# Gate and up of two SwiGLU feed-forwards as seven half products, all of down behind them

## The reference, cut to what matters

```python
def rmsnorm(x, g):
    xf = x.astype(jnp.float32)
    y = xf * lax.rsqrt(jnp.mean(xf * xf, axis=-1, keepdims=True) + EPS)
    return (y * g.astype(jnp.float32)).astype(x.dtype)

def swiglu(h, w_gate, w_up, w_down):
    return (jax.nn.silu(h @ w_gate) * (h @ w_up)) @ w_down

    x = x + 0.5 * swiglu(rmsnorm(x, g_ffn1), w1_gate, w1_up, w1_down)
    ...
    x = x + 0.5 * swiglu(rmsnorm(x, g_ffn2), w2_gate, w2_up, w2_down)
```

## Time and profile before

| what | value |
|---|---|
| median of three runs | 2342.95 us |
| time of the profiled execution | 2342.71 us |
| its span in the profile | 2340.9 us |
| PE busy in the span | 2311.1 us, 99% |
| DVE, ACT, POOL busy | 1217.3, 593.6, 59.9 us |
| moved by DMA | 169.23 MB, mean 72 GB/s |

### The profile page before, as it was taken

The page is one execution under the profiler, slowest core; times in us unless marked ns, Lnnn a source line. Parts: engine busy times, 40 slices in busy tenths (PEclk is TensorE's granted clock), DMA queues, the critical chain, the costliest instruction groups (busy, mean ns, idle before and its releaser), DMA issues.

```text
span 2340.9 us, 37286 instructions
## 1 busy us (share of the span) xinstructions
PE 2311.1 (99%) x15084; PEld 2247.2 (96%) x15084; DVE 1217.3 (52%) x2337; ACT 593.6 (25%) x1020; POOL 59.9 (3%) x100
## 2 busy tenths in 40 slices
PE   8999999999999999999999999999999999999999
PEld 7999999999999999986899987999999999999998
DVE  6544444444445775466878345265444444444445
ACT  6111211111112332246623033141111111111112
POOL 0000000000000000012400000000000000000000
PEclk9999999999999999999999999999999999999999
DMA  4111111111111321157533334311111111111111
GB/s 149 40 51 36 54 36 54 54 36 54 36 54 37 117 56 43 32 155 237 176 115 118 119 127 145 111 37 54 38 54 36 54 54 36 49 41 48 41 36 75
DMA packets 185421, 169.23 MB, mean 72 GB/s; under 512 B 6659, under 2 KB 165137, under 8 KB 185065
## 3 DMA queue, kind: packets, MB, share of 16 engines
q1 hardware_dynamic: 185329, 167.94, 23.1%
HBM read 147.98 MB, written 20.04 MB: 72 GB/s over the span
## 4 chain that ended last, share of the span: by engine, by line
PE 61%; DVE 1%; ACT 0%; DMA 0%; issue 0%; SPq 0%; DVEq 0%; ACTq 0%
PE bank L2281 17%; PE bank L2282 17%; PE bank L2283 17%; PE bank L2882 1%; PE bank L2894 1%; PE bank L2986 1%; PE bank L2715 1%; PE bank L2914 1%; PE bank L2777 1%; PE bank L2781 1%; PE bank L2787 0%; PE bank L2651 0%; DMA out_mem_k_prompt_dram<-kst 0%; PE bank L2903 0%; PE bank L2936 0%; PE bank L2924 0%
## 5 line engine op out<-in xcount | busy, mean ns | idle before, releaser
L2281 PE MATMUL bank<-h_hi,w_hi 128*128 128x352 f32 x3120 | 1011.4, 324 | 5.8 <-DVE h_lo L1361 2.8
L2282 PE MATMUL bank<-h_lo,w_hi 128*128 128x352 f32 x3120 | 1000.6, 321 | 0.0
L2283 PE MATMUL bank<-h_hi,w_lo 128*128 128x352 f32 x3120 | 1000.5, 321 | 0.0
L2281 PEld LDWEIGHTS bank<-h_hi,w_hi 128*128 128x128 f32 x3120 | 586.0, 188 | 8.4 <-DVE w_lo L1332 3.2
L2282 PEld LDWEIGHTS bank<-h_lo,w_hi 128*128 128x128 f32 x3120 | 587.3, 188 | 0.0
L2283 PEld LDWEIGHTS bank<-h_hi,w_lo 128*128 128x128 f32 x3120 | 585.8, 188 | 0.0
L1426 DVE SCALAR_TENSOR_TENSOR x<-bank,x 128x352 f32<-128x352 f32 x528 | 276.3, 524 | 187.5 <-PE bank L2283 187.3
L2281 PE MATMUL bank<-mid_hi,w_hi 128*128 128x352 f32 x1056 | 341.3, 323 | 1.2 <-DVE x L1426 1.2
L2282 PE MATMUL bank<-mid_lo,w_hi 128*128 128x352 f32 x1056 | 338.3, 320 | 0.0
L2283 PE MATMUL bank<-mid_hi,w_lo 128*128 128x352 f32 x1056 | 338.0, 320 | 0.0
L1332 DVE TENSOR_TENSOR w_lo<-w_raw,w_hi 128x1024 fp32r<-128x1024 f32 x190 | 231.1, 1244 | 48.1 <-ACT w_hi L864 46.1
(11 more groups left out here) (333 smaller groups left out, 1436.6 us busy)
## 6 DMA issues: line engine op xcount, KB each, us to landing
w_raw<-in_w_gate_dram SPq DMA_DIRECT2D x44, 512.0 KB, 3.9
w_raw<-in_w_up_dram SPq DMA_DIRECT2D x44, 512.0 KB, 4.7
w_raw<-in_w_down_dram SPq DMA_DIRECT2D x44, 512.0 KB, 4.0
w_raw<-in_w_in_dram SPq DMA_DIRECT2D x18, 512.0 KB, 4.6
x_spill<-x SPq DMA_DIRECT2D x6, 1408.0 KB, 6.2
kring<-in_cache_mem_k_dram SPq DMA_DIRECT2D x8, 1024.0 KB, 5.3
vring<-in_cache_mem_v_dram SPq DMA_DIRECT2D x8, 1024.0 KB, 5.3
dec<-acs_row SPq DMA_DIRECT2D x8, 768.0 KB, 6.5
```

The lines of the kernel that those rows point to most:

```text
L2281: eng.matmul(out, a_hi, b_hi, start=first, stop=False)
L2282: eng.matmul(out, a_hi, b_lo, start=False, stop=False)
L2283: return eng.matmul(out, a_lo, b_hi, start=False, stop=last)
```

## The change

**Seven products.** The normalised operand H (1024 features by 1056 rows) is cut in two by features and in two by rows, and each pair of weight tiles (two tiles of 128 output features, called a chunk as before) in two by input features and in two by output tile. That is a 2 x 2 by 2 x 2 block product, done in seven block products where there were eight. Each half of the rows is 528 columns, too wide for a PSUM bank of 512, so a product is made in two quarters of 264 columns (`TQ`). Products 1 to 7 of gate and of up are issued in the order `STEADY` in chunks 1 to 9, in `OPENING` in chunk 0 and `CLOSING` in chunk 10. Products 2, 3 and 6 are accumulated onto the PSUM contents of another product, so some products wait until ACT or DVE has copied a value out.

**Weights.** A chunk's gate weights are two raw tiles, and so are its up weights (four raw buffers now). GpSimd makes the weight sums in place (`sums_13`, `sums_24`); unit A is a raw tile, B and C are raw tiles whose halves were replaced by sums, D is one more half tile (128 x 512). ACT makes the high parts (`g_hi`) and DVE the low ones (`g_low`), 7 tiles' worth per chunk in place of four for gate and up.

**Operands.** The sums of halves of H need it fully normalised: x is written to DRAM (`x_keep`), GpSimd multiplies it by gain and factor in place (`normalise`, `rescale`), ACT and DVE split it, and DVE and GpSimd form the sums of halves (`second_half`, `s3_sum`). The first product no longer starts on x that isn't normalised. x is read back at the end of the products.

**Combining.** ACT copies product 1 out (`take_p1`), DVE combines the others (`take_w`, `take_u`, `take_21`, `take_12`), ACT applies the silu, GpSimd multiplies gate by up for three of the four blocks (`multiply`), DVE for the first (`act_11`). The result of every chunk is written to DRAM (`act_keep`) in four DMAs.

**Down.** All 11 chunks of down follow behind the products of all 11. Their activations are read back, ACT makes `mid_hi` and GpSimd `mid_lo` (`low_mid`). Number and shape of the down matmuls are as before (144 of 352 columns per chunk).

```diff
+HT, TQ, KH = T // 2, T // 4, KT // 2
+LAST = CHUNKS - 1
+HALF_K = KH * P
+GATE, UP = 0, 1
+ORDER = ((GATE, 1), (GATE, 2), (UP, 1), (UP, 2), (GATE, 5), (GATE, 7), (GATE, 6), (GATE, 4), (GATE, 3),
+         (UP, 5), (UP, 7), (UP, 6), (UP, 4), (UP, 3))
+STEADY = [(m, p, t) for m, p in ORDER for t in range(2)]
+OPENING = [(m, p, t) for t in range(2) for p in (1, 2) for m in (GATE, UP)] + [
+    (m, p, t) for m, p in ((GATE, 4), (UP, 4), (GATE, 5), (GATE, 7), (GATE, 6), (GATE, 3), (UP, 5), (UP, 7), (UP, 6), (UP, 3))
+    for t in range(2)]
...
-        mid_hi = sb("mid_hi", "MID", 22528, [P, 2, T], F32R)
-        mid_lo = sb("mid_lo", "MID", 30976, [P, 2, T], F32R)
-        gate = sb("gate", "MID", 39424, [P, 2, TN])
-        prod = sb("prod", "MID", 42240, [P, 2, TN])
...
+        def free(f, c, kind, m):
+            last = max(order.index((m, p, 1)) for order in (OPENING, STEADY)
+                       for p in {"A": (2,), "D": (6,), "B": (5, 4), "C": (7, 3)}[kind])
+            return NPROD * chunks(f, c) + last + 1
...
+            def act_out(f, c, q_):
+                n = chunks(f, c)
+                if q_ == 0:
+                    eng.wait_ge(g_mix, mixed(f, c, "act11", UP, 1))
+                else:
+                    eng.wait_ge(g_act, 6 * n + 2 * q_)
+                half, fi = ((0, 0), (1, 1), (1, 0), (0, 1))[q_]
+                a = slice(HT * half, HT * half + HT)
+                eng.dma_start(act_keep[:, bass.ds(2 * c + fi, 1), a], act[:, fi:fi + 1, a]).then_inc(s_act, 16)
...
+            def sums_13(f, c, m):
+                n = chunks(f, c)
+                w0, w1 = wg[2 * m], wg[2 * m + 1]
+                eng.wait_ge(g_rdy, prepared(f, c, "A", m))
+                eng.wait_ge(g_dma[m], 32 * (n + 1))
+                eng.tensor_tensor(w0[:, 0:HALF_K], w1[:, 0:HALF_K], w0[:, 0:HALF_K], ALU.subtract).then_inc(g_sum, 1)
+                eng.tensor_tensor(w1[:, 0:HALF_K], w1[:, HALF_K:2 * HALF_K], w1[:, 0:HALF_K], ALU.subtract).then_inc(g_sum, 1)
...
+            def sums_24(f, c, m):
+                n = chunks(f, c)
+                w0, w1 = wg[2 * m], wg[2 * m + 1]
+                if not (isinstance(c, int) and c == 0):
+                    eng.wait_ge(g_prod, free(f, c - 1, "D", m))
+                eng.wait_ge(g_sum, 8 * n + 2 * m + 2)
+                eng.tensor_tensor(d_f[:, m, :], w1[:, HALF_K:2 * HALF_K], w0[:, 0:HALF_K], ALU.subtract).then_inc(g_sum, 1)
+                eng.wait_ge(g_sum, 8 * n + 4 + 2 * m + 1)
+                eng.tensor_tensor(w0[:, HALF_K:2 * HALF_K], d_f[:, m, :], w0[:, HALF_K:2 * HALF_K], ALU.subtract)\
+                   .then_inc(g_sum, 1)
...
+            def multiply(f, c):
+                n = chunks(f, c)
+                for j, (half, fi, step) in enumerate(((1, 1, "22"), (1, 0, "21"), (0, 1, "12"))):
+                    eng.wait_ge(g_evict, evicted(f, c, "silu", GATE, j))
+                    for t in range(2):
+                        u_ = (p522[t][:, :], first_p[UP][:, t, :], wsum[:, t, :])[j]
+                        eng.wait_ge(g_mix, mixed(f, c, step, UP, t))
+                        out = quarter(act, half, fi, t)
+                        eng.tensor_tensor(out, u_, out, ALU.mult).then_inc(g_act, 1)
...
+            def first_half(f, t):
+                for n in range(t + 1):
+                    eng.wait_ge(s_spill[n], (16, 64)[f])
+                a, b = TQ * t, TQ * t + TQ
+                normalise(f, 0, KT, a, b, 26 * f + 10 * t)
+                eng.wait_ge(x_rb, (t + 1, spread_at(4, t) + 1)[f])
+                rescale(0, a, b)
+                rescale(KH, a, b)
...
+            def second_half(f):
+                for n in (1, 2):
+                    eng.wait_ge(s_spill[n], (16, 64)[f])
+                normalise(f, 0, KH, HT, T, 26 * f + 20)
+                eng.wait_ge(x_rb, (3, spread_at(4, 2) + 1)[f])
+                rescale(0, HT, T)
...
+            def low_mid(f, c, parity):
+                for n in range(NT):
+                    eng.wait_ge(f_mh, 3 * chunks(f, c) + n + 1)
+                    eng.tensor_tensor(mid_lo[mids(c, parity)][:, :, cols(n)], mid_raw[parity][:, :, cols(n)],
+                                      mid_hi[mids(c, parity)][:, :, cols(n)].bitcast(F32), ALU.subtract).then_inc(f_ml, 1)
...
+            def take_p1(f, c, m, t):
+                n = chunks(f, c)
+                if m == GATE:
+                    wait(eng, g_mix, mixed(f, c, "21", GATE, 1) - len(MIX))
+                else:
+                    wait(eng, g_act, 6 * n)
+                eng.wait_ge(g_prod, done(f, c, m, 1, t))
+                eng.activation(first_p[m][:, t, :], p_bank(f, m, 1, t)[:, 0:TQ], ACT.Copy).then_inc(g_evict, 1)
...
+            def silu_11(f, c, t):
+                wait(eng, s_act, 64 * chunks(f, c))
+                eng.wait_ge(g_prod, done(f, c, GATE, 2, t))
+                eng.activation(quarter(act, 0, 0, t), p_bank(f, GATE, 2, t)[:, 0:TQ], ACT.Silu).then_inc(g_evict, 1)
...
+            def strassen_chunk(f, c):
+                for t in range(2):
+                    take_p1(f, c, GATE, t)
+                for t in range(2):
+                    silu_11(f, c, t)
+                if not (isinstance(c, int) and c == 0):
+                    g_hi(f, c, "C", UP)
+                for t in range(2):
+                    take_p1(f, c, UP, t)
+                for m in range(2):
+                    g_hi(f, c + 1, "A", m)
+                strassen_rest(f, c)
...
+            def strassen_rest(f, c):
+                silu(f, c, 0)
+                g_hi(f, c + 1, "D", GATE)
+                silu(f, c, 1)
+                g_hi(f, c + 1, "B", GATE)
+                silu(f, c, 2)
+                g_hi(f, c + 1, "C", GATE)
+                g_hi(f, c + 1, "D", UP)
+                g_hi(f, c + 1, "B", UP)
...
+            def take_w(f, c, m, t):
+                eng.wait_ge(g_prod, done(f, c, m, 7, t))
+                eng.wait_ge(g_evict, evicted(f, c, "p1", m, t))
+                if m == GATE:
+                    wait(eng, g_act, 6 * chunks(f, c))
+                eng.tensor_tensor(wsum[:, t, :], first_p[m][:, t, :], p_bank(f, m, 7, t)[:, 0:TQ], ALU.subtract).then_inc(g_mix, 1)
...
+            def strassen_chunk(f, c):
+                if not (isinstance(c, int) and c == 0):
+                    g_low(f, c, "C", UP)
+                    for t in range(2):
+                        act_11(f, c, t)
+                for m in range(2):
+                    g_low(f, c + 1, "A", m)
+                combine(f, c, GATE)
+                for kind in "DBC":
+                    g_low(f, c + 1, kind, GATE)
+                combine(f, c, UP)
+                for kind in "DB":
+                    g_low(f, c + 1, kind, UP)
...
-            def ffn_gate(f, i, t):
-                gi, n = 66 * f + t + 6 * i, TURNS[t][1]
-                eng.wait_ge(f_g, gi + 1)
-                wait(eng, f_p, gi - 1)
-                eng.tensor_tensor(gate[:, t % 2, :], bank[t % 2][:, 0:TN], rb[:, cols(n)], ALU.mult).then_inc(f_gs, 1)
...
+            def product(f, c, m, p, t):
+                kind = {1: "A", 2: "A", 5: "B", 4: "B", 7: "C", 3: "C", 6: "D"}[p]
+                opening = isinstance(c, int) and c == 0
+                if t == 0:
+                    eng.wait_ge(g_rdy, prepared(f, c, kind, m))
+                if opening and f and (m, p) in ((UP, 1), (GATE, 4)):
+                    eng.wait_ge(p_free, (125 if p == 4 else 123) + t)
+                before = not opening or f
+                if (m, p) == (UP, 1) and before:
+                    eng.wait_ge(g_mix, mixed(f, c, "12", UP, t) - len(MIX))
+                elif p == 4 and before:
+                    eng.wait_ge(g_mix, mixed(f, c, "21", m, t) - len(MIX))
+                elif p == 2:
+                    eng.wait_ge(g_evict, evicted(f, c, "p1", m, t))
+                elif (m, p) == (GATE, 5):
+                    eng.wait_ge(g_evict, evicted(f, c, "silu11", GATE, t))
+                elif (m, p) == (GATE, 7):
+                    eng.wait_ge(g_mix, mixed(f, c, "act11", UP, t))
+                elif (m, p) == (UP, 7):
+                    eng.wait_ge(g_mix, mixed(f, c, "12", GATE, t))
+                elif p == 6:
+                    eng.wait_ge(g_mix, mixed(f, c, "w", m, t))
+                elif p == 3 and m == UP and isinstance(c, int) and c == LAST:
+                    eng.wait_ge(g_evict, evicted(f, c, "p5", UP, t))
+                elif p == 3:
+                    eng.wait_ge(g_mix, mixed(f, c, "22", m, t))
+                out = p_bank(f, m, p, t)[:, 0:TQ]
+                for kk in range(KH):
+                    if opening:
+                        eng.wait_ge(o_lo, 24 * f + operand_at(p, kk, t))
+                    w_h, w_l = weights(f, m, p, kk)
+                    o_h, o_l = operand(p, kk, t)
+                    mm = three(out, w_h, w_l, o_h, o_l, kk == 0 and p in (1, 5, 7, 4), kk == KH - 1, p in (2, 3, 6))
+                mm.then_inc(g_prod, 1)
```

(7 more changed lines are left out.)

1234 lines of the change are left out of this document (733 added, 501 removed).

## The result

The changed kernel takes **2471.3 us** (median of 4 runs, 2468.0 to 2475.3), the kernel before 2342.8 beside it: a ratio of 1.0548 (95% interval 1.0529 to 1.0566). That is 128 us slower, where 45 were forecast and the range ended at 2445. The profiled execution has a span of 2466.3 us, 125.4 more than that of before.

What follows compares the result with a forecast made beforehand. PE's issue rate in both feed-forwards was taken as the bound. The terms summed as 2343 - 108 + 45 + 36 + 5 + 16 + 51 = 2388 us, slower by 1.9%, with a range of 2318 to 2445.

Steps and rivals of the forecast that it cites:

- Step 1: Gate/up chunks: matmuls of 264 columns start 121.5 ns apart, 40.8 us a chunk against 45.7, -108 us for 22.
- Steps 2 and 3: Steady chunks: PE waits before up's product 6 (+45 us) and across the chunk boundary (+36), and for a load (+5).
- waits A: Before up's product 6 in 18 chunks, PE waits 2.5 us for a DVE subtraction queued behind low parts: +45 us.
- wait B: Before up's product 2, across the chunk boundary, PE waits 1.8 us for ACT's copy, 20 times: +36 us.
- a rival: Loop chunks: the clock falls at every wait, 38 times 2 us more, 2388 + 76 = 2464 us; chance 0.11.
- the +5 of part 3: Steady chunks: the load of C up reaches DVE's `take_w` of gate about when wanted, 0.3 x 18 = +5 us.
- Step 4: From products to down, twice: PE waits 6.7 us for GpSimd's first `mid_lo`, slow clock perhaps 1.5 more: +16 us.
- Step 5: Openings: operands are normalised first, so the first starts near 28 us and ends near 99; both together +51 us.
- In the down phase itself ... 0: Down phase: DVE has 15.1 us of work in 22.9, ACT 5, GpSimd 4.9, so nothing is added: 0.
- The cover holds: Chunk boundary: GpSimd's sixth multiply is done 4.2 us after the chunk's end, wait B is 0; 2320 us, chance 0.24.
- The pitch doesn't follow the columns: Gate/up matmuls: weight loads keep the pitch at 158.8 ns, 53.4 us a chunk, 2578 us in total; chance 0.03.

Runs made afterwards that it cites:

- e9: e5 with DVE's `take_w` of gate ahead of the low part A of up: 2370.6 us, ratio 1.0121.
- e5: e1 with a semaphore of its own for the first activation store, the only one the silu then waits for: 2402.4 us, ratio 1.0256.
- e2: Changed kernel with ACT's two `take_p1` copies of up ahead of the two silus, except in the openings: 2494.1 us, ratio 1.0657.
- e3: Changed kernel with the edits of e1 and e2 together: 2437.0 us, ratio 1.0400.
- e12: e3 with SP issuing gate's two weight loads of the chunk after next ahead of the last three activation stores: 2381.1 us, ratio 1.0165.
- e10: Changed kernel with the edits of e9, e8 and e6, the openings' low part C of up earlier, and chunk 0's `low_mid` before the last `multiply`: 2324.7 us.
- e6: Changed kernel with seven PSUM banks in place of three in the last two chunks of FFN1's down phase: 2460.2 us, ratio 1.0496.
- e1: Changed kernel with DVE's `take_w` of up right behind low part D of gate, ahead of B and C: 2413.3 us, ratio 1.0306.
- e8: Changed kernel with DVE scaling x in both openings; in the first, GpSimd's weight sums start only after both quarters are scaled: 2444.7 us, ratio 1.0436.

## Why the prediction was right and wrong

**Step 1, fewer columns: right.** 121.5 ns forecast, 121.3 measured where nothing waits (e9). The estimate from the rows of 288 and 352 columns carried to 264. (The range of that part is narrower than its bounds: 119.5 and 124 ns give -122 to -89 us, and not -115 to -97. Nothing came of it.)

**Steps 2 and 3, waits A and B: right in place, releaser and count, A nearly in length** (2.5 us forecast, a gap of 2.4 over the pitch), **B too long** (1.8 forecast, 1.3 measured: 27 us in all for 36). Three points were off. The clock was left out of the sum and kept for a rival; it falls behind seven of the 18 waits A and one wait B and costs 12 us in all. That this nearly makes up for B is luck, and so in part is the close total of the chunks. I gave the rival all 38 waits and 76 us: its mechanism was there, at a sixth of its price, and that its 2464 lies nearest to the 2471 measured is chance. B's cause was put down to the chain of multiplies and stores; e5 shows that the silu waited for three stores it did not need. And B was priced as if it stood alone; e5, e2 and e3 show a wait for `take_w` of gate (the +5 of part 3) under it, 1.0 us in e5 and up to 2.6 in the others, and e12 that its length there came from SP's order, in which the next loads stand behind the stores. That queue my working left out. In the changed kernel itself the +5 was right: in eight chunks of FFN1 PE's starts at G6 are 0.37 us apart in place of 0.12, 0.25 for the 0.3 forecast, since wait B has already let PE come late.

**Step 4, from products to down: right** (6.7 us forecast, 6.78 from start to start, twice). The slow matmuls it allowed for came too, 15 in FFN1 that cost 2 us, in the down phase. e10 shows that it is only order: 2.3 us from start to start with the low parts ahead of the multiplies.

**Step 5, the openings: the step that failed**, 57 of the 81 us by which the table misses. By its own terms: "GpSimd scales eight tiles (0.45 each, estimated from the 0.46 for 128 two-input elements: 3.6)" took 7.97, so PE started at 32.9 and not near 28; the two multiplies by the factors were priced rightly (4.78 for 4.7). The second quarter's low parts and the "four multiplies on DVE (2.8)" took 12.1 (43.90 to 56.02) and 7.6 beside POOL; the prediction counted the hold-up for wait B and in words for the sums, not for these. What the sum had no term for is the third store of x, asked for at 57.83 because two of DVE's copies stand behind those low parts, and the load of chunk 1's up weights, asked for only when the last low part C is made (the 9.35 us at G6, and 8.80 in FFN2). G4 was put at 60 and came at 79.8, G5 at 74 and came at 93.3, G6 at 81 and came at 110.3. The experiments give back 35 us of the 98 in e10's openings. The granted clock was 0.76 in both openings of the changed kernel; by PE's starts, slow matmuls behind the gaps cost some 8 us in the first and 9 in the second (6 and 7 in e10), and the sum had no term for them in part 5.

**"In the down phase itself ... 0": failed by 19 us at the end of FFN1.** The average was right, and the average was the mistake: VectorE's norm work for the mixer lay beside the products of the last chunk before, and lies between adds now, with three banks for PE to run ahead. e6 gets half of it back.

**The rivals.** "The cover holds" is refuted as a forecast for this kernel, but step 1's chunk of 40.8 us is e9's: VectorE at 47% and GpSimd at 37% can be hidden entirely, by order and one more semaphore and not by speed. "The pitch doesn't follow the columns" is refuted by the 121.3 ns.

The Trainium skill (SBUF — State Buffer, "Who interferes with whom"), which part 3 cites, says that a DVE instruction with two SBUF inputs contends with a GpSimd instruction that reads SBUF. For GpSimd operations with two inputs the runs agree (8.97 against 3.31 us). For GpSimd's multiply of x by the gain, which has a single tensor input, they agree only in part: beside it two low parts of weights kept their own 1.2 us each, while the half tile just behind them took 1.10 where it takes 0.69 otherwise:

```profile
66.99 2.35 DVE L1808 TENSOR_TENSOR w_lo<-w_raw,w_hi 128x1024 fp32r<-128x1024 f32 x2
```

## What to carry to other kernels

Where an engine at half load makes another wait, look at what stands ahead of the wanted instruction in its order, and at what each semaphore counts, before counting the work: here some 92 us in the chunks went, at 47% load, by moving two pairs of subtractions and splitting one semaphore. A wait that you remove may cover another on the same path, often by way of a DMA queue in which loads stand behind stores: price the next one too, and try the edits together. And price the openings and ends by their own chains, every copy, store and load in them, since a change that frees an engine in the steady part may put 50 us into a start-up that runs once.

## What the hardware showed that I had not expected

- GpSimd's multiply by a scalar per partition costs 3.8 to 4.1 ns an element (1.00 us for 264, 8.73 us for four of 528), more than its two-input operations at 2.3 to 2.5 (4.78 us for two of 1056, 1.29 for 512).
- Of 18 waits of the same length, 2.2 us, seven are followed by about 3 us at half clock (0.68 in a 5 us window) and the others by none (1.00). In e1, where the waits of a chunk are of 1.2 us and the longest is of 1.7, none is.
- Either engine can be the one that is held: eight DVE operations took 8.97 us in place of 3.31, and in e8, where DVE was under way first, one GpSimd sum took 3.81 in place of 1.29.
